# Last projection of a transformer kernel token by token, with the residual turned on TensorE and the final norm summed along the free axis

## What is computed

```python
def odd_layer(hn, w_in, w_out, rel_bias):
    cq, ck, cv, c_gate = split_cols(hn @ w_in, ODD_SPLITS)
    oc = moba_attention(cq..., ck..., cv..., rel_bias)      # 8 heads of 128, 256 tokens
    return (oc * jax.nn.silu(c_gate)) @ w_out               # [256, 1024] @ [1024, 1024]

h = h + odd_layer(hn, ...)
return rmsnorm_2(h, final_gain)     # h * rsqrt(mean(h*h, axis=-1) + EPS) * final_gain
```

## Time and profile before

| what | value |
|---|---|
| median of 3 runs | 991.48 us (991.28 to 992.29) |
| span of the profiled execution, first to last instruction | 987.1 us |
| TensorE busy | 943.5 us, 96% of the span |
| VectorE busy | 706.0 us, 72% |
| ScalarE busy | 538.3 us, 55% |
| GpSimd busy | 309.0 us, 31% |
| granted TensorE clock, mean | 0.975 |

### The profile page before, as it was taken

One profiled execution on the slowest core, in us unless ns is written; L12 is line 12 of the kernel. 1 busy time (PEld: TensorE's weight loads), 2 busy tenths in 40 slices (PEclk: granted clock), 3 DMA queues, 4 the chain that ended last, 5 costly groups with the idle time before them and its releaser, 6 DMA issues.

```text
span 987.1 us, 19548 instructions
## 1 busy us (share of the span) xinstructions
PE 943.5 (96%) x6882; PEld 871.3 (88%) x6882; DVE 706.0 (72%) x1132; ACT 538.3 (55%) x921; POOL 309.0 (31%) x272
## 2 busy tenths in 40 slices
PE   5988989999999999999979999999999999999996
PEld 5877556799999999988969999999999879899996
DVE  4997778678988777897886688555555773475664
ACT  3464655565765444654634666654444761674645
POOL 1942122237997111120051288640110000330012
PEclk9898999999999999999979999999999998999999
DMA  9856175168878777788615676555555332255521
GB/s 351 292 182 239 42 226 171 47 218 309 309 271 275 284 267 279 244 324 283 225 61 171 234 256 214 186 176 190 171 192 182 130 95 98 86 172 173 169 87 43
DMA packets 57052, 195.60 MB, mean 198 GB/s; under 512 B 6303, under 2 KB 9791, under 8 KB 56736
## 3 DMA queue, kind: packets, MB, share of 16 engines
q1 hardware_dynamic: 55312, 192.36, 56.7%
q0 software_dynamic: 1680, 2.44, 1.1%
HBM read 192.65 MB, written 1.07 MB: 196 GB/s over the span
## 4 chain that ended last, share of the span: by engine, by line
PE 85%; DVE 9%; ACT 2%; issue 2%; DMA 1%; POOL 0%; SPq 0%; DVEq 0%; ACTq 0%
PE bank L526 24%; PE bank L527 24%; PE bank L528 24%; DVE w_lo L1576 2%; PE bank L791 1%; PE bank L925 1%; PE bank L951 1%; PE bank L624 1%; PE bank L782 1%; DMA x<-x_in 1%; PE bank L824 1%; PE bank L633 1%; PE bank L879 1%; DVE ada_raw L1678 1%; DVE ada_raw L1591 1%
## 5 line engine op out<-in xcount | busy, mean ns | idle before, releaser
L1576 DVE TENSOR_TENSOR w_lo<-raw,w_hi 128x1024 fp32r<-128x1024 f32 (+1 forms) x261 | 340.0, 1304 | 108.0 <-ACT w_hi L1146 106.1
L1146 ACT ACTIVATE w_hi<-raw 128x1024 fp32r<-128x1024 f32 (+1 forms) x261 | 272.4, 1044 | 174.4 <-PE bank L528 166.4
L526 PE MATMUL bank<-act_hi,w_hi 128*128 128x258 f32 (+1 forms) x872 | 251.5, 288 | 0.0
L527 PE MATMUL bank<-act_lo,w_hi 128*128 128x258 f32 (+1 forms) x872 | 248.0, 284 | 0.0
L528 PE MATMUL bank<-act_hi,w_lo 128*128 128x258 f32 (+1 forms) x872 | 247.5, 284 | 0.0
L526 PEld LDWEIGHTS bank<-act_hi,w_hi 128*128 128x128 f32 x872 | 166.1, 190 | 3.3 <-issue 2.8
L527 PEld LDWEIGHTS bank<-act_lo,w_hi 128*128 128x128 f32 x872 | 166.1, 190 | 1.0 <-issue 1.0
L528 PEld LDWEIGHTS bank<-act_hi,w_lo 128*128 128x128 f32 x872 | 166.1, 190 | 0.0
L528 PE MATMUL bank<-hid_hi,w_lo 128*128 128x256 f32 x512 | 143.4, 280 | 0.0
L526 PE MATMUL bank<-hid_hi,w_hi 128*128 128x256 f32 x512 | 142.8, 279 | 0.0
L527 PE MATMUL bank<-hid_lo,w_hi 128*128 128x256 f32 x512 | 142.8, 279 | 0.0
(11 more groups left out here) (349 smaller groups left out, 1812.7 us busy)
## 6 DMA issues: line engine op xcount, KB each, us to landing
raw<-weights SPq DMA_DIRECT2D x247, 512.0 KB, 3.6
ada_raw<-ada SPq DMA_DIRECT2D x88, 512.0 KB, 4.8
raw<-weights SPq DMA_DIRECT2D x14, 384.0 KB, 4.3
ada_more<-ada SPq DMA_DIRECT2D x8, 512.0 KB, 6.4
bias<-bias_by_distance SPq DMA_DIRECT2D x1, 2048.0 KB, 9.1
x<-x_in SPq DMA_DIRECT2D x1, 1024.0 KB, 7.3
ctx<-ctx_in SPq DMA_DIRECT2D x1, 1024.0 KB, 9.5
out<-result SPq DMA_DIRECT2D x4, 256.0 KB, 2.7
```

What stands on the lines that cost most here:

```text
L526: pe.matmul(dst, w[0], a[0], start=start, stop=False)
L527: pe.matmul(dst, w[0], a[1], start=False, stop=False)
L1146: act.activation(w_hi[:, slot, 0:width_of(c)], raw[:, slot, 0:width_of(c)], ACT.Copy).then_inc(weight_hi, 1)
L1576: dve.tensor_tensor(w_lo[:, slot, 0:w], raw[:, slot, 0:w], w_hi[:, slot, 0:w].bitcast(fp32), ALU.subtract).then_inc(weight_lo, 1)
```

## The change

The last projection is done token by token: for each of two token tiles (tt) and each half of the features (f) one bank holds 128 tokens x 512 features. The activations of a head are stationary, 512 weight columns move. A chunk holds two k tiles of one half. The residual is put into the bank first by four transposing products of `x` with the identity (`residual_turned`), and the projection accumulates on it. The chunks are used in the order of the host's new layout: half 0 k 0 to 3, half 1 k 0 to 3, half 0 k 4 to 7, half 1 k 4 to 7. The conversions of chunks 4 to 7 on ScalarE and VectorE come between the last heads and right behind them. ScalarE squares each bank and sums it along the free axis. VectorE multiplies the first half by the gain, held as a row on all partitions (`final_row`, loaded by SyncE). The root and its reciprocal are columns with one value for each token; ScalarE scales the first half by it, VectorE the second half with the gain in one instruction. SyncE stores four pieces of 128 x 512. TensorE's sums and spreading and GpSimd's sum of squares go. The result leaves token-major.

```diff
-    ("odd_g", [1] * 8), ("odd_k", [1] * 2), ("odd_v", [0, 2]), ("odd_q", [1] * 8), ("odd_out", [1] * 8),
+    ("odd_g", [1] * 8), ("odd_k", [1] * 2), ("odd_v", [0, 2]), ("odd_q", [1] * 8),
+    ("odd_out", [0] * 5 + [2, 0, 2]),
...
-RAW = {name: 8 * i for i, name in enumerate(["ffn0_in", "gm_in", "ffn1_in", "even_in", "odd_in", "final"])}
+RAW = {name: 8 * i for i, name in enumerate(["ffn0_in", "gm_in", "ffn1_in", "even_in", "odd_in"])}
...
+OUT_BANKS_OF = ((0, 1), (3, 7))
...
-            result = sb("result", [P, KT, S], fp32, odd)
+            result = sb("result", [P, 2, D], fp32, odd)
+            final_row = sb("final_row", [P, D], fp32, odd)
+            final_tok = sb("final_tok", [P, 2, 5], fp32, odd)
...
+        def final_bank(tt, f):
+
+            return bank[OUT_BANKS_OF[f][tt]]
...
-            for j in range(KT // 2):
-                sp.wait_ge(out_ready, j + 1)
-                sp.dma_start(out[:, 2 * j:2 * j + 2, :], result[:, 2 * j:2 * j + 2, :]).then_inc(out_written, 16)
-            sp.wait_ge(out_written, 16 * (KT // 2))
+            sp.wait_ge(blocks.scores, 2 * H)
+            sp.dma_start(final_row[:], c_rows[2].partition_broadcast(P)).then_inc(table_in, 16)
+            for tt in range(2):
+                for ready, before, half in ((raw_hi, 5 * KT, slice(0, 512)), (out_ready, 0, slice(512, D))):
+                    sp.wait_ge(ready, before + tt + 1)
+                    sp.dma_start(out[:, tt, half], result[:, tt, half]).then_inc(out_written, 16)
+            sp.wait_ge(out_written, 16 * 4)
...
-            def split_product(dst, w, a, start, stop, weights_move=False):
+            def split_product(dst, w, a, start, stop, weights_move=False, shared=False):
 
 
                 if weights_move:
                     w, a = a, w
-                pe.matmul(dst, w[0], a[0], start=start, stop=False)
-                pe.matmul(dst, w[0], a[1], start=False, stop=False)
-                return pe.matmul(dst, w[1], a[0], start=False, stop=stop)
+                pe.matmul(dst, w[0], a[0], start=start, stop=False, skip_group_check=shared)
+                pe.matmul(dst, w[0], a[1], start=False, stop=False, skip_group_check=shared)
+                return pe.matmul(dst, w[1], a[0], start=False, stop=stop, skip_group_check=shared)
...
-            late("odd_out", odd_o, range(2), range(4), a_wait=odd_o_wait)
+            def residual_turned(f):
+
+                for tt in range(2):
+                    for j in range(4):
+                        pe.matmul(final_bank(tt, f)[:, j * P:(j + 1) * P], x[:, 4 * f + j, tt * P:(tt + 1) * P], ident,
+                                  is_transpose=True, start=j == 0, stop=False, skip_group_check=True)
+
+            def out_chunk(i, f, k0):
+
+                pe.wait_ge(weight_lo, chunk0["odd_out"] + i + 1)
+                for tt in range(2):
+                    tok = slice(tt * P, (tt + 1) * P)
+                    for k in (k0, k0 + 1):
+                        if tt == 0:
+                            pe.wait_ge(split_lo, split0["odd_o"] + k + 1)
+                        last = split_product(final_bank(tt, f)[:], weight(chunk0["odd_out"] + i, (k - k0) * 512, 512),
+                                             (oo_hi[:, k, tok], oo_lo[:, k, tok]), False, k == KT - 1,
+                                             weights_move=True, shared=True)
+                    if tt == 1 or k0 == KT - 2:
+                        last.then_inc(matmul_steps, 1)
+
+            residual_turned(0)
+            out_chunk(0, 0, 0)
             beat_turn(blocks, 6, prob_o)
             block_values(5)
-            late("odd_out", odd_o, range(2, 4), range(4))
-            late("odd_out", odd_o, range(2), range(4, 5), a_wait=odd_o_wait)
+            residual_turned(1)
+            out_chunk(1, 0, 2)
             beat_turn(blocks, 7, prob_o)
             block_values(6)
-            late("odd_out", odd_o, range(2, 4), range(4, 5))
-            late("odd_out", odd_o, range(4), range(5, 6), a_wait=odd_o_wait)
+            out_chunk(2, 1, 0)
             block_values(7)
-            late("odd_out", odd_o, range(4), range(6, 7), a_wait=odd_o_wait)
-            late("odd_out", odd_o, range(4), range(7, 8), a_wait=odd_o_wait)
-            late("odd_out", odd_o, range(4, 8))
-            pe.wait_ge(square_sums, 6 * (KT - 2))
-            for tt in range(2):
-                pe.matmul(bank[4 + 2 * tt][:, 0:1], square_sum[:, tt * P:(tt + 1) * P], mean[:, 0:1],
-                          start=True, stop=False)
-            pe.wait_ge(squared, squares_before(6) + KT)
-            for tt in range(2):
-                last = pe.matmul(bank[4 + 2 * tt][:, 0:1], sq[:, KT - 1, tt * P:(tt + 1) * P], mean[:, 0:1],
-                                 start=False, stop=True)
-            last.then_inc(sums_ready, 1)
-            pe.wait_ge(tok_scale, 3)
-            for tt in range(2):
-                last = pe.matmul(bank[5][:, tt * P:(tt + 1) * P], rstd_tok[:, 2 + tt:3 + tt].to_broadcast([P, P]),
-                                 ident, start=True, stop=True)
-            last.then_inc(sums_ready, 1)
+            out_chunk(3, 1, 2)
+            out_chunk(4, 0, 4)
+            out_chunk(5, 0, 6)
+            out_chunk(6, 1, 4)
+            out_chunk(7, 1, 6)
...
                 block_beat(b)
+                convert(chunk0["odd_out"] + b - 3)
+            convert(chunk0["odd_out"] + 7)
             act.activation(std[:, S:S + 1], eps[:], ACT.Sqrt)
-            for g in range(KT):
-                convert(chunk0["odd_out"] + g + 4)
-                square_residual("odd_out", g)
-                act.activation(result[:, g, :], x[:, g, :], ACT.Copy, scale=V("final_gain", g, 1)).then_inc(raw_hi, 1)
-            act.wait_ge(sums_ready, 8)
-            act.activation(rstd_tok[:, 0:1], bank[4][:, 0:1], ACT.Sqrt, bias=eps[:])
-            act.activation(rstd_tok[:, 1:2], bank[6][:, 0:1], ACT.Sqrt, bias=eps[:]).then_inc(std_tok, 1)
+
+            def final_square(tt, f):
+
+                act.wait_ge(matmul_steps, after_group[group0["odd_out"] + 2 * f + tt])
+                act.activation(sq[:, 4 * f + 2 * tt:4 * f + 2 * tt + 2, :].rearrange("p a b -> p (a b)"), final_bank(tt, f)[:], ACT.Square,
+                               accum_out=final_tok[:, tt, f:f + 1]).then_inc(squared, 1)
+
+            final_square(0, 0)
+            final_square(1, 0)
+            for tt in range(2):
+                final_square(tt, 1)
+                act.wait_ge(squared, squares_before(6) + 3 + tt)
+                act.wait_ge(gained, KT + 2 * tt + 2)
+                act.activation(final_tok[:, tt, 3:4], final_tok[:, tt, 1:2], ACT.Sqrt, scale=1.0 / D,
+                               bias=final_tok[:, tt, 2:3]).then_inc(std_tok, 1)
+                act.wait_ge(tok_scale, tt + 3)
+                act.activation(result[:, tt, 0:512], result[:, tt, 0:512], ACT.Copy,
+                               scale=final_tok[:, tt, 4:5]).then_inc(raw_hi, 1)
...
             for b in (7, 8, 9):
                 block_logits(b)
                 block_rest(b)
-            for g in range(KT):
-                residual("odd_out", g)
-                convert(chunk0["odd_out"] + g + 4)
-            dve.wait_ge(std_tok, 3)
-            dve.reciprocal(rstd_tok[:, 2:4], rstd_tok[:, 0:2]).then_inc(tok_scale, 1)
-            dve.wait_ge(sums_ready, 9)
-            for j in range(KT // 2):
-                dve.wait_ge(raw_hi, RAW["final"] + 2 * j + 2)
-                pair = result[:, 2 * j:2 * j + 2, :]
-                dve.tensor_tensor(pair, pair, bank[5][:, 0:S].unsqueeze(1).to_broadcast([P, 2, S]),
-                                  ALU.mult).then_inc(out_ready, 1)
+                convert(chunk0["odd_out"] + b - 3)
+            convert(chunk0["odd_out"] + 7)
+            dve.wait_ge(table_in, 64)
+            for tt in range(2):
+                dve.wait_ge(squared, squares_before(6) + tt + 1)
+                dve.tensor_tensor(result[:, tt, 0:512], final_bank(tt, 0)[:], final_row[:, 0:512],
+                                  ALU.mult).then_inc(gained, 1)
+                dve.tensor_scalar(final_tok[:, tt, 2:3], final_tok[:, tt, 0:1], 1.0 / D, EPS, ALU.mult,
+                                  ALU.add).then_inc(gained, 1)
+            for tt in range(2):
+                dve.wait_ge(std_tok, tt + 3)
+                dve.reciprocal(final_tok[:, tt, 4:5], final_tok[:, tt, 3:4]).then_inc(tok_scale, 1)
+                dve.wait_ge(tok_scale, tt + 3)
+                dve.scalar_tensor_tensor(result[:, tt, 512:D], final_bank(tt, 1)[:], final_tok[:, tt, 4:5],
+                                         final_row[:, 512:D], ALU.mult, ALU.mult).then_inc(out_ready, 1)
...
-            sum_squares(6)
...
-        "final_gain": cols(a["final_gain_2"]), "gla_b_up": cols(a["gla_b_up_2"][0]),
...
-        chunks_of(a["w_out_odd_2"][0]),
+        chunks_by_token(a["w_out_odd_2"][0], 512)[[0, 1, 4, 5, 2, 3, 6, 7]],
...
```

(14 more changed lines are left out.)

## The result

| | before | after |
|---|---|---|
| median of 4 runs | 991.88 us (991.28 to 994.74) | 982.1 us (977.54 to 984.38) |
| span of the profiled execution | 987.1 | 982.6 |
| granted TensorE clock, mean | 0.975 | 0.972 |
| VectorE, ScalarE, GpSimd busy | 706.0, 538.3, 309.0 | 703.0, 535.9, 301.8 |

The ratio is 0.9892 (0.9864 to 0.9921). The sign was right, the size was not.

A forecast was written before the change was run, and what follows sets the result against it. TensorE's products and what follows its last instruction bound the kernel. 1.1 us less at TensorE and 3.0 behind it make 4.1: 991.48 - 4.1 = 987.4 us, with 8 in 10 for 986.2 to 990.0.

The forecast's parts named there:

- Side edits: `final_row` load, narrower `vecs`, third row of `c_rows`, host's weight order: claimed to cost nothing any row would show.
- for a drift elsewhere in the kernel: Remaining chance given to a time change outside the part the forecast priced; no size; 3 in 100.
- priced stage: From the start of head 7's scores to the end of the span: 4.1 us less.
- Products: Last projection on TensorE: 96 products of 512 columns at 0.230 replace 192 of 256 columns; 0.54 us less.
- Residual: 16 transposed products of 128 columns added on TensorE at 0.11 us each: +1.76 us.
- Rival (a): Turned residual products pay their full duration of 273 ns: +2.6 us, 990.0 us; 4 in 100.
- Stalls: TensorE's waits between head 7's scores and its end, longest for `w_lo`, disappear: -2.33 us.
- Rival (b): Moved conversions hold up the last heads, so TensorE stands still as long as before: +2.3 us, 989.7; 5 in 100.
- TensorE's sum: TensorE's end after products, residual and stalls: -0.54 + 1.76 - 2.33 = -1.11 us, to 977.25.
- rival (c): TensorE's clock falls in the last stretch: 993.3 us if long (3 in 100), 990.1 if short (3 in 100).
- Tail: Work after TensorE's last product, from squares to stores, shortens by 3.0 us; last transfer issued at 980.0.
- Outside the span: Time not in the profiled span, 991.48 - 987.1 = 4.4 us, taken to stay as it is.

The follow-up runs named there:

- e9: Kernel before with only `final_gain` taken out of `vec`, which narrows by 32 bytes, and loaded into its own tile: 985.81 us, ratio 0.9947 to before.
- e3: Changed kernel with 32 unused bytes behind `vec`, putting most later tiles back at their old addresses: 985.54 us, ratio 0.9949 to the kernel before.
- e2: Changed kernel, unchanged, run again: 981.61 us, ratio 0.9906 to the kernel before.
- e1: Kernel before, unchanged, run against itself: 991.37 us, ratio 1.0015.
- e18: Changed kernel with 160 unused bytes behind `vec`, timed in full: 977.25 us, ratio 0.9862 to the kernel before.
- e5: Changed kernel without the turned residual (16 transposing products): 980.44 us, ratio 0.989 to the kernel before.
- e6: Changed kernel with the conversions of chunks 4 to 7 moved back behind the heads, table load ahead of them: 984.87 us, ratio 0.9945 to the kernel before.
- e15: Changed kernel with 160 unused bytes behind `vec`, run once for its trace: 973.93 us.

## Why the prediction was wrong, point by point

**The step that failed** is in *Side edits*: that the narrower `vecs` costs nothing on the chip that any row would show, and with it the prediction's last sentence, that up to 950 "I give the change nothing there". The narrower tile shifted every tile behind it by 32 bytes against the ring of weights, and the pitch of the products changed: 576 x 3 = 1728 products of 258 columns at 1.61 / 742 = 0.0022 less make 3.7 us, 1536 on `hid` at 0.85 / 767 = 0.0011 less make 1.7, and 576 on `s` take some 0.4 more (0.1163 to 0.1170). The sum is 5.0, from single profiles; e9 measured 5.2 (3.1 to 7.3) with that edit alone, and e3 against e2 4.3 (some 2.6 either way). It is shown by adding the effect to the old kernel and by taking it from the new one. No rival held it; the 3 in 100 "for a drift elsewhere in the kernel" had no mechanism and no size. With it the forecast would have been 987.4 - 5 = 982.4, beside the 982.1 measured; that these are so close is partly luck, since the stage came out 0.7 smaller than forecast by the profiles. The text had counted a tile that is narrower as less work, and not as another place for all others.

**The priced stage** came out at 3.4 less by the two profiles (3.1 if e1 and e2 stand for the two kernels), and at 5.1 +- 1.8 by e3, where 4.1 was forecast. That e3's time gives 1.7 more than the stage does in the traces is within its interval and has no other explanation here.

- *Products*, -0.54 forecast. The pitch is 0.234 and not the 0.230 of the earlier trace rows, so 96 of them take 22.46: -0.16. The row was of the same form with other operands, and the pitch moves with where they lie: these same products take 0.2271 each in e18 (58 steps in 13.17) and 0.2324 in e3, where `oo_hi` lies elsewhere against `w_hi`. The 192 products of before are no fixed number either, as e1 shows: from the scores to the last product it takes 27.72 and not 28.15.
- *Residual*, +1.76 forecast: 1.74 by e5, 0.87 for eight in the chain. Rival (a), the full duration, is out. The Trainium skill, page "TensorE: Matmul & The Clock Gate", section "Part 4: PE-mode transpose", gives about 275 ns; the runs agree with that as the duration of one (272 ns) and not as the cost of one in a stream (0.109 us).
- *Stalls*, -2.33 forecast: TensorE runs without a gap from 950 to its end (26.53 us busy to 976.53), and e6 brings 2.14 back by moving the conversions alone. Rival (b) did not occur.
- *TensorE's sum*, -1.11 forecast: 28.15 - 27.29 = 0.86 by starts. The terms, -0.16 + 1.74 and the 2.3 that before stood still, make -0.7; the last product, wider by 0.1, stands between the two ways of counting.
- *The clock*, rival (c), stayed at 1.00 from 950 to 977.
- *Tail*, -3.0 forecast, -2.6 measured. The order is as forecast, down to the last square waiting behind the scaling of token tile 0. The sizes are each a little larger: the scaling took 0.72 for the 0.60 taken (the bound was 0.70), the last multiplication 0.75 for 0.69, an issue 0.39 for 0.33. The landings, 2.4 to 2.8, were those of the earlier trace rows.

**Outside the span** the prediction left 4.4 us. That was really about 1.8, as every profiled run with its own time shows (984.38 - 982.6 = 1.8; 1.8 to 2.0 in all of them); the rest was an execution shorter than the median. It did no harm, since only the difference was used, but it should have warned that two single executions can't be compared to 3 us.

**Open.** Why the distance matters is not shown; the runs say that it does, for which tiles and with what period, and nothing about why some streams have a second pitch at the same distance. Nor is shown that it is the distance to `w_hi` and `w_lo` and not to another tile ahead of `vec`, nor which half of the split matters. Other distances, and those of each tile by itself, were not tried, so 192 for `hid` with 64 for `act` is the best of those tried and not known to be the best.

## What to carry to other kernels

A change of a tile's width moves every tile allocated behind it, so compare the pitch of an untouched stream of products in both traces before a gain or a loss is put down to the edit; an unused tile of the missing width is the control that tells the two apart. Profile the same kernel twice before a pitch is relied on, for some streams have two. In a kernel that TensorE bounds, a scan of a few paddings between the weights and the activations, within 256 bytes, costs one line each and was worth here as much as a rewritten projection. And where several stores end the kernel, look whether the transfers already run without a gap: then issuing them closer together only lengthens their landing, and an earlier first store is what is left to try, which no run here did.

## What the hardware showed that was not expected

- The pitch of an fp32r product of 256 columns, in one stretch, was 0.1134, 0.1167, 0.1178, 0.1187 and 0.1200 us at distances of 192, 32, 64, 160 and 96 bytes modulo 256 between the stationary and the moving tile, at clock 1.00: 6% from end to end (86.94 to 92.04 us for 768).
- In that stretch it is the same to 0.01 us in 768 products across kernels and runs, though whole runs of one kernel spread by 6 us (987.99 to 993.94 for before in 23 runs).
- Other streams have two pitches at one distance, in executions of the very same kernel: 43.30 and 44.99 us for 382 steps (e18, e15), 10.65 and 11.07 for 94 (e1, before).
- Four stores of 256 KB issued within 2.2 us landed after 2.4 to 2.8 us, issued within 1.3 us after 2.4 to 3.3, with the DMA engines busy without a gap for 3 us at 295 to 385 GB/s.
